# Two transformer blocks on one core: the kernel's start and the entry of its second block rearranged

## The reference, cut to what matters

```python
# block one
h = rmsnorm(x, norm_mix_g); proj = h @ w_in              # 7 parts of 1024 columns
...                                                       # gating, convolution, two projections, w_out
hf = rmsnorm(x, norm_ff_g); z = relu(hf @ w_ff1); x = x + (z * z) @ w_ff2
x = rmsnorm(x, norm_final_g)
# block two
mod = silu(c) @ w_ada + b_ada                             # shifts, scales, gates
hn = rms_norm(x, g_norm1) * (1 + scale1) + shift1
proj = hn @ w_in_2                                        # q, k, v, o, gates, q, k, v
h_m = mlstm_chunkwise(...)                                # decays from cumulated gates
h_a = moba_attention(...)                                 # one block of 256 keys: causal attention
x = x + gate1 * (concat(h_m, h_a) @ w_out_2)
x = x + gate2 * hierarchical_moe(...)                     # 32 experts, 2 per token
return rms_norm(x, g_final)
```

## Time and profile before

| | |
|---|---|
| median of three runs | 1069.55 us |
| profiled execution, its own time | 1072.3 us |
| its span, first to last instruction | 1070.5 us |
| PE busy | 1031.2 us, 96% of the span |
| DVE busy | 504.0 us, 47% |
| ACT busy | 407.3 us, 38% |
| chain that ended last, by engine | PE 85%, DMA 9%, DVE 3%, ACT 2%, issue 1% |
| moved by DMA | 327.89 MB, mean 306 GB/s |

### The profile page before, as it was taken

The page is one execution under the profiler, slowest core; times in us unless marked ns, Lnnn a source line. Parts: engine busy times, 40 slices in busy tenths (PEclk is TensorE's granted clock), DMA queues, the critical chain, the costliest instruction groups (busy, mean ns, idle before and its releaser), DMA issues.

```text
span 1070.5 us, 13772 instructions
## 1 busy us (share of the span) xinstructions
PE 1031.2 (96%) x5644; PEld 697.7 (65%) x5644; DVE 504.0 (47%) x703; ACT 407.3 (38%) x635; POOL 22.2 (2%) x42
## 2 busy tenths in 40 slices
PE   5999999999999999989999999999999999999885
PEld 4888878888999999789888644444444444444332
DVE  4477768887987754557856512121211111111112
ACT  5744553435544444455754322222222222222112
POOL 1000000010000000100000000000000000000000
PEclk9999999999999999889999999999999999999998
DMA  9977447976788753264443999999999999999993
GB/s 331 349 257 260 171 157 273 324 269 237 263 314 297 266 173 143 95 236 158 157 166 134 370 409 422 421 420 422 421 422 420 420 421 422 422 421 421 422 420 128
DMA packets 86307, 327.89 MB, mean 306 GB/s; under 512 B 5744, under 2 KB 5776, under 8 KB 61536
## 3 DMA queue, kind: packets, MB, share of 16 engines
q1 hardware_dynamic: 84896, 323.45, 78.1%
q0 software_dynamic: 1344, 3.50, 1.0%
HBM read 325.88 MB, written 1.05 MB: 305 GB/s over the span
## 4 chain that ended last, share of the span: by engine, by line
PE 85%; DMA 9%; DVE 3%; ACT 2%; issue 1%; SPq 0%; DVEq 0%; ACTq 0%
PE bank L982 17%; PE bank L1005 8%; PE bank L541 8%; PE bank L538 8%; PE bank L542 8%; PE bank L671 5%; PE bank L566 4%; PE bank L570 4%; PE bank L567 4%; DMA es<-in_w_expert_up 3%; DMA e_wlo<-in_w_expert_up 3%; PE bank L676 3%; PE bank L1018 3%; DMA raw<-in_w_expert_up 3%; PE bank L950 3%; PE bank L991 1%
## 5 line engine op out<-in xcount | busy, mean ns | idle before, releaser
L1546 DVE TENSOR_TENSOR wlo<-raw,whi 128x2048 fp32r<-128x2048 f32 x90 | 205.7, 2289 | 105.6 <-ACT whi L1071 105.2
L1071 ACT ACTIVATE whi<-raw 128x2048 fp32r<-128x2048 f32 x90 | 171.6, 1912 | 97.2 <-PE bank L542 40.3
L2154 DVE SCALAR_TENSOR_TENSOR YS<-bank,wsl,gate2q 128x512 f32<-128x512 f32 x32 | 24.0, 751 | 217.8 <-PE bank L1005 217.8
L982 PE MATMUL bank<-raw,XT 128*64 128x512 f32 x360 | 119.8, 597 | 0.0
L982 PE MATMUL bank<-es,XT 128*64 128x512 f32 x328 | 112.3, 594 | 3.8 <-DMA es<-in_w_expert_up 2.8
L541 PE MATMUL bank<-wlo,hh 128*128 128x512 f32 x224 | 88.3, 394 | 3.2 <-DVE wlo L1546 3.2
L538 PE MATMUL bank<-whi,hh 128*128 128x512 f32 x224 | 88.6, 396 | 1.2 <-ACT whi L1071 1.2
L542 PE MATMUL bank<-whi,hl 128*128 128x512 f32 x224 | 87.9, 392 | 0.0
L982 PEld LDWEIGHTS bank<-es,XT 128*64 128x64 f32 x328 | 33.7, 137 | 72.6 <-issue 71.3
L982 PE MATMUL bank<-e_whi,XT 128*64 128x512 f32 x168 | 76.1, 596 | 2.7 <-DMA e_wlo<-in_w_expert_up 2.7
L982 PE MATMUL bank<-e_wlo,XT 128*64 128x512 f32 x168 | 76.2, 596 | 0.0
(11 more groups left out here) (371 smaller groups left out, 1955.5 us busy)
## 6 DMA issues: line engine op xcount, KB each, us to landing
raw<-in_w_in SPq DMA_DIRECT2D x42, 1024.0 KB, 5.5
raw<-in_w_expert_up SPq DMA_DIRECT2D x33, 1024.0 KB, 22.7
raw<-in_w_ff SPq DMA_DIRECT2D x32, 1024.0 KB, 5.3
es<-in_w_expert_gate SPq DMA_DIRECT2D x31, 1024.0 KB, 22.5
raw<-in_w_ada SPq DMA_DIRECT2D x24, 1024.0 KB, 5.6
e_whi<-in_w_expert_gate SPq DMA_DIRECT2D x21, 1024.0 KB, 22.9
e_wlo<-in_w_expert_up SPq DMA_DIRECT2D x21, 1024.0 KB, 25.0
es<-in_w_expert_down SPq DMA_DIRECT2D x21, 1024.0 KB, 26.1
```

Source lines behind the costliest of these rows:

```text
L982: m = e.matmul(b[64 * w:64 * w + 64, :], K.XT[j // 4 % 2][:, k, j % 4, :], K.weights(halves[w])[:, 512 * c:512 * c + 512], start=k == 0, s ...
L1071: e.activation(whi[n % RING][:, :], raw[h.raw][:, :], ACT.Copy).then_inc(S["hi"], 1)
L1546: e.tensor_tensor(wlo[n % RING][:, :], raw[h.raw][:, :], whi[n % RING][:, :].bitcast(F32), ALU.subtract).then_inc(S["lo"], 1)
```

## The change

- Start: only the identity's columns of `cst` are loaded ahead of x, x's halves count on semaphores of their own, weight half 0 comes in two DMAs and the rest of `cst` behind it. PE first multiplies a tile of ones four times, then transposes token half 0 and token half 1 into banks that now hold chunks k and k + 4. ACT and DVE alternate a chunk of `hh`/`hl` with a quarter of weight half 0.
- Halves 0, 1 and 73 (`PIECED`) are split by quarters with semaphores `hi_p`, `lo_p`; the dense products wait chunk by chunk. `dense_half` is changed as `dense_turned` is. Where `ready` is given, PE waits for `x_hi` and for `x_lo` at the matmuls that read them.
- Entry: transposes of token half 0 go ahead of the feed-forward's last quarter, those of token half 1 around `last_rows`; the column sums go behind, half before and half after `Rb`; the dummies go. `hi(73)` in quarters comes ahead of `ada_cols_in(6)`; `root(5)` follows it.
- The decays' products are put between `KA`'s first chunks and at its middle.

```diff
@@ -21,6 +21,7 @@
+PIECED = (0, 1, 73)
@@ -332,6 +333,10 @@
+    def landed(self, h, c):
+        return (self.S[f"first{c // 2}"], 16) if h.i == 0 else (self.S[f"raw{h.raw}"], h.loaded)
@@ -369,7 +374,7 @@
-            other(f"xT{k}", "x_lo", 2 * k + 2)
+            other(f"xT{k}", "x_lo", k + 5)
@@ -524,21 +529,30 @@
+    def part(side, n, c):
+        if n in PIECED and c < 3:
+            e.wait_ge(S[f"{side}_p"], 3 * PIECED.index(n) + c + 1)
+        elif n in PIECED or c == 0:
+            e.wait_ge(S[side], n + 1)
@@ -549,35 +563,47 @@
-    def dense_turned(use, n, xh, xl, ready=None, mid=None):
+    def dense_turned(use, n, xh, xl, ready=None, mid=None, each=None):
         free(use)
...
             s = (n + hf) % RING
-            e.wait_ge(S["hi"], n + hf + 1)
             for c in range(4):
                 k = 4 * hf + c
+                part("hi", n + hf, c)
                 if ready:
-                    e.wait_ge(S[ready[0]], ready[1](k))
+                    e.wait_ge(S["x_hi"], ready(k))
                 for q in range(4):
...
                     e.matmul(o, w_h, xh[:, k, :], start=k == 0 and q % 2 == 0, stop=False, skip_group_check=True)
+                    if ready and q == 0:
+                        e.wait_ge(S["x_lo"], ready(k))
                     e.matmul(o, w_h, xl[:, k, :], start=False, stop=False, skip_group_check=True)
-                    if c == 0 and q == 0:
-                        e.wait_ge(S["lo"], n + hf + 1)
+                    if q == 0:
+                        part("lo", n + hf, c)
                     m = e.matmul(o, w_l, xh[:, k, :], start=False, stop=k == 7, skip_group_check=True)
+                if c < 3 and each:
+                    each(k)
             m.then_inc(S["used"], 1)
...
+    e.wait_ge(S["warm"], 1)
+    for _ in range(4):
+        e.matmul(bank[3][:, :], K.gate1b[:, 0:128], K.gate1b[:, 128:640], start=True, stop=True)
+    for t in range(2):
+        e.wait_ge(S[f"l_x{t}"], (32, 16)[t])
+        for k in range(4):
+            for c in range(2):
+                o, i = 256 * c + 128 * t, 512 * c + 128 * k
+                m = e.transpose(K.at[f"xT{k}"][0][:, o:o + 128], K.x[:, t, i:i + 128], C("ident"))
+            if t:
+                m.then_inc(S["turned"], 1)
+    dense("V0", 0, K.hh, K.hl, (lambda k: SPLIT["h"] + k + 1))
     e.wait_ge(S["l_cst"], 16)
-    e.wait_ge(S["l_x"], 32)
-    for k in range(4):
-        turn(f"xT{k}", K.x, k)
-    dense("V0", 0, K.hh, K.hl, ("x_lo", lambda k: SPLIT["h"] + k + 1))
     dense("V1", 2, K.hh, K.hl)
@@ -685,8 +711,22 @@
     e.wait_ge(S["zl"], 16)
+    def turn_x2(t, ks):
+        for k in ks:
+            for c in range(2):
+                o, i = 256 * c + 128 * t, 256 * k + 128 * c
+                m = e.transpose(K.at[f"x2T{k}"][0][:, o:o + 128], K.x[:, t, i:i + 128], C("ident"))
+            if t:
+                m.then_inc(S["turned"], 1)
     for t in range(2):
         for q in range(2):
+            if t and q:
+                for k in range(4):
+                    free(f"x2T{k}")
+                e.wait_ge(S["x"], X_AT["2"] + 2)
+                turn_x2(0, range(4))
             m0 = ff2_half(7, 0, 70, (t,), (q,))
@@ -696,16 +736,14 @@
-    def last_cols():
-
-        free("adac6")
-        e.wait_ge(S["ada_st"], 8 * 9 + 8)
-        for g in range(6, 10):
+    def last_cols(gs):
+        for g in gs:
             for c in range(4):
...
                              start=True, stop=True)
-        m.then_inc(S["ada_c"], 1)
+        return m
@@ -722,19 +760,21 @@
-    last_cols()
+    e.wait_ge(S["x"], X_AT["2"] + 3)
+    turn_x2(1, (0, 1))
+    last_rows()
     e.wait_ge(S["x"], X_AT["2"] + 4)
-    for k in range(4):
-        turn(f"x2T{k}", K.x, k)
-    last_rows()
-    stay_busy(1, "Rb")
+    turn_x2(1, (2, 3))
+    free("adac6")
+    e.wait_ge(S["ada_st"], 8 * 9 + 8)
+    last_cols((6, 7))
     free("Rb")
...
     m.then_inc(S["gates_mm"], 1)
-    stay_busy(2, "QK0")
-    dense_turned("QK0", 72, K.nh, K.nl, ("x_lo", lambda k: SPLIT["n"] + k + 1))
+    last_cols((8, 9)).then_inc(S["ada_c"], 1)
+    dense_turned("QK0", 72, K.nh, K.nl, (lambda k: SPLIT["n"] + k + 1))
     free("gates")
@@ -756,12 +796,15 @@
     e.wait_ge(S["F"], 3)
-    for h in range(4):
-        free(f"decay{h}")
-        e.matmul(K.at[f"decay{h}"][0][:, 0:256],
-                 K.cst[0:4, CST["ident"] + h:CST["ident"] + h + 1].to_broadcast([4, 128]), K.R["M"][:, :], start=True,
-                 stop=True).then_inc(S["dec_mm"], 1)
-    dense_turned("KA", 78, K.nh, K.nl)
+    def decay(h):
+        if h < 4:
+            free(f"decay{h}")
+            e.matmul(K.at[f"decay{h}"][0][:, 0:256],
+                     K.cst[0:4, CST["ident"] + h:CST["ident"] + h + 1].to_broadcast([4, 128]), K.R["M"][:, :],
+                     start=True, stop=True).then_inc(S["dec_mm"], 1)
+    dense_turned("KA", 78, K.nh, K.nl, None, lambda: decay(3), decay)
     dense("VA", 80, K.nh, K.nl)
@@ -1070,6 +1113,13 @@
+    def hi_piece(n, c):
+        h, o = K.mm[n], slice(512 * c, 512 * c + 512)
+        e.wait_ge(*K.landed(h, c))
+        if n >= RING and c == 0:
+            e.wait_ge(S["used"], n - RING + 1)
+        e.activation(whi[n % RING][:, o], raw[h.raw][:, o], ACT.Copy).then_inc(S["hi" if c == 3 else "hi_p"], 1)
     def two(b):
@@ -1099,16 +1149,19 @@
     e.activation(K.sc[:, :], K.vec[:, VEC["c"]:VEC["c"] + 8], ACT.Silu).then_inc(S["silu_c"], 1)
-    for k in range(4):
-        e.wait_ge(S["turned"], TURNED["x"] + k + 1)
-        for c in range(2):
-            e.activation(K.hh[:, 2 * k + c, :], K.at[f"xT{k}"][0][:, 256 * c:256 * c + 256], ACT.Copy,
-                         scale=V("g_mix", 2 * k + c)).then_inc(S["x_hi"], 1)
-        if k == 1:
-            hi(0)
-    hi(1)
+    for q in range(8):
+        e.wait_ge(S["turned"], TURNED["x"] + q % 4 + 1)
+        if q > 3:
+            e.wait_ge(S["x_lo"], SPLIT["h"] + q - 3)
+        e.activation(K.hh[:, q, :], K.at[f"xT{q % 4}"][0][:, 256 * (q // 4):256 * (q // 4) + 256], ACT.Copy,
+                     scale=V("g_mix", q)).then_inc(S["x_hi"], 1)
+        if q < 4:
+            hi_piece(0, q)
+    for c in range(4):
+        hi_piece(1, c)
     hi(2)
-    e.wait_ge(S["l_x"], 32)
+    e.wait_ge(S["l_x0"], 32)
+    e.wait_ge(S["l_x1"], 16)
     squares(K.x[:, 0, :], 0, K.junk3[:, 0, :])
@@ -1286,11 +1339,12 @@
         e.activation(K.nh[:, q, :], K.nf[:, q, :], ACT.Identity, bias=K.ada_cols[:, q:q + 1]).then_inc(S["x_hi"], 1)
+    for c in range(4):
+        hi_piece(73, c)
+    root(5, 24)
     ada_cols_in(6)
-    hi(73)
+    hi(74)
     ada_rows_in(10)
-    hi(74)
-    root(5, 24)
     e.wait_ge(S["turned"], TURNED["x2"] + 4)
@@ -1546,6 +1600,15 @@
+    def lo_piece(n, c):
+        h, o = K.mm[n], slice(512 * c, 512 * c + 512)
+        if c < 3:
+            e.wait_ge(S["hi_p"], 3 * PIECED.index(n) + c + 1)
+        else:
+            e.wait_ge(S["hi"], n + 1)
+        e.tensor_tensor(wlo[n % RING][:, o], raw[h.raw][:, o], whi[n % RING][:, o].bitcast(F32),
+                        ALU.subtract).then_inc(S["lo" if c == 3 else "lo_p"], 1)
     def two(b):
@@ -1556,17 +1619,18 @@
+    e.memset(K.gate1b[:, 0:640], 1.0).then_inc(S["warm"], 1)
     e.memset(K.ws[64:128, :, 0:64], 0.0).then_inc(S["ws_z"], 1)
     e.wait_ge(S["l_vec"], 16)
-    for k in range(4):
-        for q in (2 * k, 2 * k + 1):
-            e.wait_ge(S["x_hi"], SPLIT["h"] + 2 * k + 2)
-            e.scalar_tensor_tensor(out=K.hl[:, q, :], in0=K.at[f"xT{k}"][0][:, 256 * (q % 2):256 * (q % 2) + 256],
-                                   scalar=V("g_mix", q), in1=K.hh[:, q, :].bitcast(F32), op0=ALU.mult,
-                                   op1=ALU.subtract).then_inc(S["x_lo"], 1)
-        if k == 1:
-            lo(0)
-    lo(1)
+    for q in range(8):
+        e.wait_ge(S["x_hi"], SPLIT["h"] + q + 1)
+        e.scalar_tensor_tensor(out=K.hl[:, q, :], in0=K.at[f"xT{q % 4}"][0][:, 256 * (q // 4):256 * (q // 4) + 256],
+                               scalar=V("g_mix", q), in1=K.hh[:, q, :].bitcast(F32), op0=ALU.mult,
+                               op1=ALU.subtract).then_inc(S["x_lo"], 1)
+        if q < 4:
+            lo_piece(0, q)
+    for c in range(4):
+        lo_piece(1, c)
     lo(2)
@@ -1814,8 +1879,10 @@
                                    op1=ALU.subtract).then_inc(S["x_lo"], 1)
-    inv_rms(5, 24, D)
-    lo(73)
+    for c in range(4):
+        lo_piece(73, c)
+    e.wait_ge(S["sd"], 5)
+    e.reciprocal(stat(24, 2), stat(24, 2)).then_inc(S["rs"], 1)
     lo(74)
@@ -2274,6 +2341,12 @@
         o = h.before
+        if h.i == 0:
+            for c in range(2):
+                e.dma_start(K.raw[0][:, 1024 * c:1024 * c + 1024].rearrange("p (c n) -> p c n", c=2),
+                            h.src[:, 2 * c:2 * c + 2, :]).then_inc(S[f"first{c}"], 16)
+            e.dma_start(K.cst[:, CW["ident"]:NCST], A["cst"][:, CW["ident"]:NCST]).then_inc(S["l_cst"], 16)
+            return
         if o:
@@ -2291,9 +2364,9 @@
```

(6 more changed lines are left out.)

25 lines of the change are left out of this document (14 added, 11 removed).

## The result

In the first four runs the changed kernel took 1054.81 to 1057.68 us, median 1055.18, against 1069.33 for the kernel before beside it: ratio 0.9866, 95% interval 0.9841 to 0.9890. Later, in five more rounds on one chip, it was 1056.00 against 1069.29, ratio 0.988 (0.9856 to 0.9904). Over all runs the medians are 1055.56 (10 runs) and 1069.35 (47 runs of before in the later comparisons): a gain of 13.8 us. These two pooled medians are what the experiments are set against. Forecast: 1052, in a range of 1048 to 1058, with 17.7 us of gain. So the direction and the range were right and the size was 3.9 us too large.

What follows compares the result with a forecast made beforehand. PE's chain of waits was taken to bound the front, the expert-weight stream the end, following the front. Terms 5.9 + 9.8 + 1.7 + 0.3 = 17.7 us, off the median 1069.55, gave 1051.9, said as 1052; range 1048 to 1058.

Steps and rivals of the forecast that it cites:

- The frame: Whole kernel: if PE's front half moves earlier by X, buffer releases, expert-weight stream and end move by X.
- Start, 5.9 us: Kernel start through V0: earlier x, warm-up and quartered weight splits end V0 sooner, gaining 5.9 us, bounds 2.5 to 7.
- single waits: Chunks at pa0, pb0, wo0, ff0: waiting separately for x_hi and x_lo gains 0.3 us, bounds 0 to 0.6.
- Entry, 9.8 us: Entry of block two to QK0's end: reordered work and quartered half 73 gain 9.8 us, bounds 6 to 12.4.
- Decays, 1.7 us: KA's first four chunks: spreading the decay products removes a half-clock stretch, gaining 1.7 us, bounds 0 to 2.
- 1: Entry: one more half-clock stretch over QK0 and a late Rb, gain 6 instead of 9.8, time 1056; chance 0.14.
- 2: Start: gain 2 instead of 5.9, as dummies hold PE, x lands no earlier, lo(3) late; 1056, chance 0.10.
- 3: End: the expert stream keeps its absolute place and does not follow the front; some 1069, chance 0.04.
- 4: QK0, gates and QK1: without dummies the clock stays at half throughout, 25.9 us more; 1075, chance 0.02.

Runs made afterwards that it cites:

- old start: Changed kernel with the earlier kernel's start (constants in one transfer, no warm-up, weight halves 0 and 1 split whole), entry and decays kept: 1061.37 us.
- old entry: Changed kernel with the entry of block two as before (transposes behind the last quarter, columns together, dummies back, half 73 split whole), start and decays kept: 1063.88 us.
- after, again: Changed kernel unedited, run again beside the kernel before for a second profile: median 1056.00 us in 6 runs.
- before, again: Kernel before the change, unedited, run again for a second profile and its spread: median 1069.96 us in 12 runs, second profiled execution 1066.54.
- block variant: Changed kernel with its four decay products in one block ahead of KA, as before the change: 1055.53 us.
- filled entry: Changed kernel with two busy-keeper products where PE idles at the entry, 256 columns ahead of Rb and 512 ahead of QK0: 1056.19 us.
- dense entry: Changed kernel with columns 6, 7 ahead of the last transposes, 8, 9 moved into QK0, and busy-keeper products before Rb and between Rb and QK0: 1055.20 us.

## Why the prediction was right in kind and 3.9 us too large

- **The frame** held: the end follows the front. "VA to last issue" is 514.7 to 516.3 us whatever the front does, PE's waits for expert weights hardly grew (from 2.8 to 3.4 us in this group, for 14.6 us of gain). In the changed kernel's profile, against the earlier trace rows:

```profile
PE bank L1025 <- DMA es<-in_w_expert_up: 3.4, 2, 2.5
```

- **Start, 5.9 us** (bounds 2.5 to 7). The quarter's end moved by 6.1 and 5.3 in the two pairs of profiles, and putting the old start back costs 5.4 us. The first two include the 0.3 forecast for single waits, which no run shows by itself. The steps came as said: warm-up to 7.6 (7), first `hi` piece done 9.9 (9.4), first `lo` piece 10.6 (10.1), last matmul of V0 21.25 (near 21), and PE waits for no `lo` in V1. What I had not seen is which part does it: pieces, not early x or warm-up. I had weighed the Trainium skill's advice of 1 MiB or more per DMA (DMA: Bandwidth & Descriptors, Rules for kernel authors). At x's 2.1 us per 512 KB the second piece of the first half would have landed at 11.5; ACT took it at 11.05 without waiting, so cutting the half in two cost nothing that can be seen here:

```profile
11.05 0.64 ACT L1121 ACTIVATE whi<-raw 128x512 fp32r<-128x512 f32 x1
```

- **Entry, 9.8 us** (6 to 12.4). 10.4 in the first pair, 8.3 in the medians of the old entry against after. `nf` 5.42 us after the quarter (5.3 forecast), QK0's end 21.7 after it (21.4), no stop, half clock for 6.8 us (3.5 to 6.9). Every step right, against that one execution. With the old start's 5.4 to 5.8 us the old entry's 8.3 make up the whole 13.8: next to nothing is left for the decays.
- **Decays, 1.7 us** (0 to 2): failed. Two errors: "spread over KA's first four chunks they cost the same 2.0 us" is 3.2; and the half-clock stretch behind the block, 1.7 in the sum, is 1.5 (41.56 less 40.06) and is not there in every execution. The term is +0.4 or -1.1, outside my bounds in the second case.
- **The step from the sum to the forecast**: failed. The text says that 17.7 off the profiled execution is 1054.6, notes that this execution lay 2.75 us above the median, and then takes the whole 17.7 off the median. But 10.2 us of half clock at the entry and 3.4 behind the decays, which the second profile of before does not have, are what made that execution long, and they are what two terms of the sum remove. With the second profile of each kernel the difference is 12.0. The median's gain, 13.8, lies between 12.0 and 14.6. Against the pooled 1055.56 the forecast is 3.6 us low; 1054.6 would have been 1.0 low. Within the first pair the sum is 3.1 too large (17.7 against 14.6): 0.6 too little for the entry, 1.3 too much for the decays, and the tail's 2.4. That the time still fell inside the range owes more to the range's width above the forecast (6 us) than to this step.
- **The tail**: not in the sum. In the profiled pair it takes back 2.4 us. The row that shows it is a group of PE's products near the last weight issue, which waits 2.50 us and then runs at half clock (granted from 1006.8 to 1010.2; 5.35 us, where such a group took 3.65 earlier):

```profile
1006.28 5.35 PE L1025 MATMUL bank<-es,XT 128*64 128x512 f32 x16 [2.50 <-DMA es<-in_w_expert_up]
```

It is not owed to the change: "after, again" has 45.9 us there, as "before, again" has. So it does not explain the medians.
- The rivals. 1 (the clock holds the entry down) did not come: one half-clock stretch, 3.4 or 6.8 us, as in the forecast. 2: the warm-up did hold PE until 7.6 and gains nothing that can be told, but the pieces gave the start its gain all the same. 3 and 4 are out: the end followed, and full clock was back by 443.6.
- The Trainium skill (TensorE: Matmul & The Clock Gate, Part 4) says transposes don't count as busy for the clock; I had set against it. The runs leave it mixed. Without warm-up, turns from 5.00 to 8.65 and matmuls from 9.04 ran at half until 14.2; with the old start, turns from 5.42 to 9.65 brought no full clock either. That speaks for the page. In both profiles of the kernel before, full clock was granted from 11.9 and 11.8 after nothing but turns. Which it is stays open.

## What to carry to other kernels

Before a sum made on one profiled execution is taken off a median, look how that execution differs from the median (its mean clock above all), and whether the terms remove just what made it long; then the two are not independent, and the sum belongs to its own execution. Price a small product between big ones by the time from its issue to the regained rhythm of the flow, not by its share of a block. Where an engine waits at the start for a whole tile to be converted, cut the conversion first; here V0's end moved by 5.4 us with the pieces, by 1.3 at most with the warm-up and by 0.9 with the smaller first transfer.

## Not expected of the hardware

- The same instructions took 32.1 or 27.8 us in one stretch, with the same waits, and only the granted clock differs (0.79 against 0.94). The kernel before has executions from 1066.2 to 1075.4 us, and they sort by their mean clock.
- Half clock does not double the spacing of the matmuls of 256 columns: 0.12 us apart at full clock and 0.21 in the block variant's KA, so 3.4 us of it cost 1.5 and not 1.7.
- Filling all idle time of PE at the entry did not keep the clock up (filled entry), and moving half of the one-column products away, with products of 512 columns in their place, did (dense entry, one profile each).
